# The up-projection with tokens stationary and 512 weight columns moving, block borders crossed one token tile at a time, and the modulation tiles spread anew

## The reference, cut to what matters

```
cond = silu(c)
mod  = (cond @ ada_w[layer] + ada_b[layer]).reshape(B, 9, 1024)
h = modulate(rmsnorm(x, g), sh, sc)
x = x + 0.5 * gate * swiglu(h, w13, w2)     # D_FF = 2816, four times in all
x = x + gate2 * mix                         # layer 0: attention, layer 1: pooling
```

## Time and profile before

| quantity | value |
|---|---|
| span of the profiled execution | 1045.7 us |
| time of that execution | 1047.53 us |
| median of the runs | 1046.29 us |
| PE busy | 955.1 us (91%) |
| DVE busy | 739.9 us (71%) |
| ACT busy | 434.0 us |
| POOL busy | 123.0 us |
| share of PE in the chain that ended last | 82% |
| mean DMA rate | 229 GB/s |

### The profile page before, as it was taken

One profiled execution on the slowest core, in us unless ns is written; L12 is line 12 of the kernel. 1 busy time (PEld: TensorE's weight loads), 2 busy tenths in 40 slices (PEclk: granted clock), 3 DMA queues, 4 the chain that ended last, 5 costly groups with the idle time before them and its releaser, 6 DMA issues.

```text
span 1045.7 us, 15095 instructions
## 1 busy us (share of the span) xinstructions
PE 955.1 (91%) x6240; PEld 866.6 (83%) x6240; DVE 739.9 (71%) x791; ACT 434.0 (42%) x529; POOL 123.0 (12%) x182
## 2 busy tenths in 40 slices
PE   1599999998979597999999989999999879999997
PEld 1499999986857466999999979999998779999996
DVE  4888787857897846887878478878784675454543
ACT  1343434443526544444443344343443445434341
POOL 1111111002451102111110021101110010000000
PEclk9999999998989788999999989999999889999999
DMA  9989888867624106899797567989794225564621
GB/s 339 373 306 327 305 313 291 298 177 234 231 96 153 40 2 228 281 331 345 272 324 261 192 221 258 330 284 333 265 346 158 81 82 198 184 198 165 215 67 61
DMA packets 147140, 239.58 MB, mean 229 GB/s; under 512 B 16128, under 2 KB 108160, under 8 KB 146944
## 3 DMA queue, kind: packets, MB, share of 16 engines
q1 hardware_dynamic: 126480, 166.81, 48.2%
q0 software_dynamic: 19440, 71.31, 17.7%
q10 hardware_dynamic: 1152, 0.49, 0.2%
HBM read 237.54 MB, written 1.05 MB: 228 GB/s over the span
## 4 chain that ended last, share of the span: by engine, by line
PE 82%; DVE 11%; ACT 2%; issue 2%; POOL 1%; DMA 1%; POOLq 0%; ACTq 0%; SPq 0%; DVEq 0%
PE ps L1151 55%; PE ps L1193 7%; PE ps L1194 7%; PE ps L1197 7%; DVE x L814 1%; DVE xn L810 1%; DVE lo L722 1%; PE ps L1213 1%; PE ps L1206 1%; DVE acc L768 1%; DMA x<-in_x 1%; POOL rstd L385 1%; DVE xn L768 1%; PE ps L1443 1%; DVE arena L944 1%
## 5 line engine op out<-in xcount | busy, mean ns | idle before, releaser
L1151 PE MATMUL ps<-hT_hi,hi 128*128 128x256 f32 x1408 | 405.2, 288 | 4.4 <-DVE hT_lo L831 4.4
L1151 PE MATMUL ps<-hT_lo,hi 128*128 128x256 f32 x1408 | 401.8, 285 | 0.0
L1151 PE MATMUL ps<-hT_hi,lo 128*128 128x256 f32 x1408 | 401.6, 285 | 0.0
L722 DVE TENSOR_TENSOR lo<-raw,hi 128x2048 fp32r<-128x2048 f32 (+1 forms) x110 | 244.3, 2221 | 126.1 <-ACT hi L461 125.7
L1151 PEld LDWEIGHTS ps<-hT_hi,hi 128*128 128x128 f32 x1408 | 273.5, 194 | 9.4 <-issue 7.1
L1151 PEld LDWEIGHTS ps<-hT_lo,hi 128*128 128x128 f32 x1408 | 273.6, 194 | 3.5 <-issue 1.2
L461 ACT ACTIVATE hi<-raw 128x2048 fp32r<-128x2048 f32 (+1 forms) x106 | 200.6, 1892 | 181.9 <-PE ps L1151 165.0
L1151 PEld LDWEIGHTS ps<-hT_hi,lo 128*128 128x128 f32 x1408 | 273.3, 194 | 0.0
L1193 PE MATMUL ps<-hi,u_hi 128*128 128x512 f32 x344 | 135.3, 393 | 2.8 <-DVE u_lo L742 2.6
L1194 PE MATMUL ps<-lo,u_hi 128*128 128x512 f32 x344 | 135.2, 393 | 0.0
L368 POOL DMA_DIRECT2D ada<-in_ada_w x132 | 71.6, 543 | 439.7 <-DVE acc L768 160.6
(11 more groups left out here) (138 smaller groups left out, 823.6 us busy)
## 6 DMA issues: line engine op xcount, KB each, us to landing
raw<-in_ff_w SPq DMA_DIRECT2D x264, 512.0 KB, 6.5
ada<-in_ada_w POOLq DMA_DIRECT2D x132, 512.0 KB, 7.1
raw<-in_w_in SPq DMA_DIRECT2D x24, 512.0 KB, 5.0
arena<-in_ada_w SPq DMA_DIRECT2D x4, 1024.0 KB, 18.9
raw<-in_w_out SPq DMA_DIRECT2D x8, 512.0 KB, 4.4
raw<-in_ada_w SPq DMA_DIRECT2D x2, 1024.0 KB, 15.1
arena<-in_b_rpb SPq DMA_DIRECT2D x16, 128.0 KB, 4.7
x<-in_x SPq DMA_DIRECT2D x2, 512.0 KB, 7.5
```

The costliest lines, as they stand in the source:

```text
L722: ins = V.tensor_tensor(lo, src, hi.bitcast(F32), ALU.subtract)
L1151: ins = mm(out, a, b, start=first and m == 0, stop=last and m == len(pairs) - 1, skip_group_check=shared)
```

## The change

The change has six parts.

1. `w13` now holds 128 tokens stationary (`hT`) and moves 512 weight columns, 256 of each half of the SwiGLU (two runs in the piece). A piece takes 24 products of 128 x 512 instead of 48 of 128 x 256. Since the result now has the tokens on the partitions, `u` must be transposed: `u_transpose` adds four 128 x 128 transposes per pair, and the split of `u` reads PSUM.
2. The last pair of a block is done tile by tile: w13 and w2 of tile 0, then its residual and norm while TensorE works on tile 1. The first pair of the next block starts with tile 0, and tile 1's norm transposes stand within it. The mixer's input projection and the output projection are ordered likewise.
3. `lo` is written over `raw`, `hi13` has four slots and the pieces seven (three of them in the arena while it is idle). A slot is reloaded once TensorE has used the piece. `raw2` and `hi2` have four slots.
4. The modulation tiles: block 0 takes 40 in pairs 1 to 9, block 1 takes 40 in pairs 2 to 9 (five a pair), block 2 takes 32, block 3 the last 8. The sums are transposed in two halves in one bank.
5. Of the first 16 tiles TensorE takes four as products with a column of `cond` (`mod_columns`), and VectorE twelve, the last two in halves.
6. The eight GpSimd instructions on the bias are gone; a 128 x 64 window is built at the start, and VectorE applies it with one minimum per token tile (`bias_window`) at steps 10 and 11 of the input projection.

```diff
-                for kk in range(4):
-                    k = 4 * half + kk
-                    hh, hl = hT_hi[:, k, :], hT_lo[:, k, :]
-                    for ab in range(2):
-                        for q in range(2):
-                            ins = three(dst, ((wh, hh), (wh, hl), (wl, hh)), k == 0 and q == 0, k == KT - 1, shared=True)
+                for t in tiles:
+                    tok = slice(t * P, (t + 1) * P)
+                    for kk in range(4):
+                        k = 4 * half + kk
+                        hh, hl = hT_hi[:, k, tok], hT_lo[:, k, tok]
+                        ins = three(ps[:, pair_bank(f, p) + t, :].rearrange("p (m c) -> p m c", m=2),
+                                    ((hh, wh[:, :, kk, :]), (hh, wl[:, :, kk, :]), (hl, wh[:, :, kk, :])),
+                                    k == 0, k == KT - 1)
...
+            def u_transpose(f, p, tiles=range(TT)):
+                for t in tiles:
+                    for q in range(2):
+                        dst = ps[:, z + t, q * P:(q + 1) * P] if last else ps[:, z, q * 256 + t * P:q * 256 + t * P + P]
+                        ins = nc.tensor.transpose(dst, u_buf[:, t, q * P:(q + 1) * P], ident[:, :])
...
+                    w13(f, p, 0)
+                    u_transpose(f, p - 1)
+                    w13(f, p, 1)
+                    w2(Q0 + 2 * p - 2)
+                    w2(Q0 + 2 * p - 1)
...
+                w13(f, LAST, 0, [0])
+                u_transpose(f, LAST - 1)
+                w13(f, LAST, 1, [0])
+                w2(Q0 + NC - 4, tiles=[0], done=None)
+                u_transpose(f, LAST, [0])
+                w2(Q0 + NC - 3, tiles=[0], done=None)
+                w2(Q0 + NC - 2, tiles=[0], done=None)
+                w2(Q0 + NC - 1, tiles=[0], last=True, done=y0_done)
+                w13(f, LAST, 0, [1])
+                w13(f, LAST, 1, [1])
+                    norm_transpose(s_out, 0)
+                w2(Q0 + NC - 4, tiles=[1])
+                u_transpose(f, LAST, [1])
+                w2(Q0 + NC - 3, tiles=[1])
+                w2(Q0 + NC - 2, tiles=[1])
+                w2_last(Q0 + NC - 1)
...
+ADA_COUNT = [{1: 4, 2: 4, 3: 5, 4: 4, 5: 5, 6: 4, 7: 5, 8: 4, 9: 5}, {p: 5 for p in range(2, 10)},
+             {p: 4 for p in range(2, 10)}, {2: 4, 3: 4}]
+PE_TILES = ((5, 7), (3, 5))
...
+            def bias_window(t):
+                b = bias[:, t, :, :, :].rearrange("p h r c -> p (h r) c")
+                V.tensor_tensor(b, b, window[:, :].unsqueeze(1).to_broadcast([P, B_HEADS * ROWS, GRID_W]), ALU.min
+                                ).then_inc(bias_done, 1)
-                    nc.gpsimd.affine_select(out=low, in_=low, compare_op=ALU.is_ge, fill=NEG,
-                    nc.gpsimd.affine_select(out=high, in_=high, compare_op=ALU.is_ge, fill=NEG,
```

More of the change, by code:

```diff
@@ L269, in load_win @@
[L269 to L279, removed]
@@ new lines, in load_piece, with load_until @@
+            def load_piece(n):
+                if BEFORE[n] >= 0:
+                    sp.wait_ge(unit_used, BEFORE[n] + 1)
+                for m, src in enumerate(piece_srcs(n)):
+                    rows, cols = src.shape[1:]
+                    c0 = m * rows * cols
+                    sp.dma_start(unit_src(n)[0][:, c0:c0 + rows * cols].rearrange("p (k c) -> p k c", c=cols), src
+                                 ).then_inc(raw13_in[SLOT[n]], 16)
+            loaded = [4]
+            def load_until(n):
+                while loaded[0] < PIECES and BEFORE[loaded[0]] <= n:
+                    load_piece(loaded[0])
+                    loaded[0] += 1
@@ L286, in load_w2 @@
             def load_w2(f, q):
                 n = NC * f + q
[L288 to L297, removed]
+                if n >= 4:
+                    sp.wait_ge(w2_used, n - 3)
@@ L780, in diag, with mod_out @@
+            def mod_out(g):
+                for half in range(2):
+                    mod_half(g, half, MOD_BANK + half)
             def diag(g, k, scale, dst=diag_buf):
@@ L1128, in _ @@
             split_lo(2 * FFN_PAIR[3] + 1)
+            norm_split(5, 0)
+            residual(5, 1, unit_used, 2 * POOL_PAIR + 2, part=1)
+            norm_scale(5, 1)
+            norm_split(5, 1)
             ffn(3)
-            residual(6, w2_used, 4 * NC, halves=4)
         @block.tensor
@@ L1243, in ffn @@
-                if f < 3:
-                    mod_sum(FFN_MODS[f] + 4, spare_bank(f, PAIRS - 1))
-                w2(Q0 + 20, tiles=[0], done=None)
-                w2(Q0 + 21, tiles=[0], last=True, done=y0_done)
-                w2(Q0 + 20, tiles=[1])
-                w2_last(Q0 + 21)
+                Q0, s_in, s_out = NC * f, SUB_OF_FFN[f], SUB_OF_FFN[f] + 1
+                for t in range(TT):
+                    w13(f, 0, 0, [t])
+                    w13(f, 0, 1, [t], between=(lambda: norm_transpose(s_in, 1)) if f and t == 0 else None)
@@ new lines, in ffn, with pool_average @@
+                w2(Q0 + NC - 2, tiles=[1])
+                w2_last(Q0 + NC - 1)
+            def pool_average(kt, first, last):
+                for j in range(first, last):
+                    t0 = kt * (P - max(WINDOWS) // 2)
+                    c0 = (j % 2) * 256
+                    ins = mm(ps[:, POOL_BANK[j // 2], c0 + t0:c0 + SEQ], xn[:, kt, j * P:(j + 1) * P],
+                             avg[:, j // 2, kt, t0:], start=kt == 0 and j % 2 == 0, stop=kt == 1, skip_group_check=True)
+                    if j % 2 and kt:
+                        ins.then_inc(pool_ps, 1)
@@ L1278, in proj @@
                         t0_done = None
+                    if between is not None and kk == 1:
+                        between()
                 if done:
@@ L1374, in _ @@
             n0 = 2 * WIN_PAIR
+            for t in range(TT):
+                for w in range(2):
+                    proj(n0 + w, lambda t: ps[:, 4 + t, :], tiles=[t], hs=lambda t, k: HLO[1] + 8 * t + k + 1,
+                         start=w == 0, stop=w == 1, done=t == 1, t0_done=seg_ps if (t, w) == (0, 1) else None,
+                         between=(lambda: norm_transpose(1, 1)) if (t, w) == (0, 1) else None)
             for w in range(12):
```

996 lines of the change are left out of this document (585 added, 411 removed).

## The result

| kernel | median of the runs | ratio to before, 95% interval |
|---|---|---|
| before | 1046.7 us (4 runs) | 1 |
| after | 1018.2 us (1016.1 to 1021.4, 4 runs) | 0.9742 (0.9716 to 0.9768) |

The change made the kernel 2.6% faster. My sum had 1010.0 us for the profiled execution; it took 1016.1, with a span of 1014.0. The median lies 9.7 us above my 1008.5. That is inside the whole range (994 to 1027), but at its own forecast's upper edge: 1018.2 stands just outside both 1001 to 1017 and 1000 to 1018. Stretch by stretch, all but one came within 1.6 us of the forecast, and the mixer's early stretch missed it by 9.8. First the busy time by stretch, of the kernel after, with the columns of the earlier trace rows: us, PE, PEld, DVE, ACT, POOL, granted clock, DMA share, GB/s.

What follows compares the result with a forecast made beforehand. TensorE was taken to bound the blocks, with gains also at borders and in the mixer. Terms summed to 37.5 us off the profiled 1047.5, so 1010.0; median forecast 1008.5 us, whole range 994 to 1027.

Steps and rivals of the forecast that it cites:

- 1001 to 1017 and 1000 to 1018: Kernel time in us: the forecast case, given chance 0.60, and the likeliest case's own range.
- the mixer's early stretch: Mixer from the end of its first two pieces to the piece behind the first scores: 54.8 us before, gain 11.5.
- TensorE's pace in the blocks: Blocks' middle pairs: w13 products 0.227 us each, a pair 16.9 us instead of 17.0, gain 2.3 us.
- rival 1: Blocks: w13's two-run operand costs as much as two products, 1035.5 us; chance 0.09 together with slower transposes of u, 1030.5.
- The transposes of `u`: Each pair in the blocks: four transposes of u inside the running stream cost about 0.48 us.
- Rivals 2 and 3: 2: VectorE or modulation-tile ring bounds blocks 0 and 1, 1025, chance 0.10; 3: u's round trip stands bare, 1056, 0.05.
- the borders: Block 0 to mixer, block 1 to 2, mixer to block 1, block 2 to 3: gains of 7.3, 7.7, 3.3, 4.0 us.
- the start: Program start: four tiles leave VectorE, the first weights' DMA and last tiles set the pace; gain 1.3 us.
- TensorE's own work in it is 41.9 ... 43.3: a gain of 11.5: Mixer up to the scores: without GpSimd's slowing VectorE is no later than TensorE; 54.8 us falls to 43.3.
- stays above 50 us: Sign that the prediction is wrong: the mixer's stretch to the scores stays above 50 us.
- The minima: Mixer: VectorE's two minima over 2048 elements replace GpSimd's cuts and cost 1.1 us.

Runs made afterwards that it cites:

- experiment 5: Kernel after, with each of the four transposes of u in a pair done twice: 1035.8 us, ratio 0.9907.
- Experiment 6: Kernel after, with tile 1's w13 again ahead of tile 0's w2 products in a block's last pair: 1040.6 us, ratio 0.9957.
- experiments 9 and 10: Kernel after with early bias loads and block 3's first split later: 1009.3 us; the same without modulation tiles on TensorE: 1012.6 us.
- experiment 3: Kernel after with early bias loads, the eight bias cuts back on GpSimd and VectorE's minima gone: 1020.0 us, ratio 0.9748.
- experiments 1 and 2: Kernel after, 1: bias table's loads issued early, ahead of the mixer's weight pieces, 1012.1 us; 2: those loads left out, 1012.7 us. Both ratio 0.9682.
- experiment 4: Kernel after, with SyncE issuing each pair's two w2 chunks ahead of the w13 pieces: 1059.2 us, ratio 1.0130.

## Why the prediction was right, and where it was not

**Right: TensorE's pace in the blocks.** 24 products of 512 columns take 5.44 to 5.49 us a piece, 0.227 each, with the moving operand in two runs: rival 1 is out. The transposes of `u` cost 0.44 us for four where I had 0.48. That rests on experiment 5, not on the trace alone. The Trainium skill ("TensorE: Matmul & The Clock Gate", Part 4, PE-mode transpose) has about 275 ns for one transpose in another kernel; here, between products, it is 0.11 us, and the measurement decides. Rivals 2 and 3 did not come about: TensorE is busy 141.0 of 141.0 us in block 1. Rival 2 has one trace in block 0: the wait of 2.2 us at 103.08 is for VectorE's part of a modulation sum.

**Right: the borders.** 7.6, 7.9, 3.9 and 3.6 us, against 7.3, 7.7, 3.3 and 4.0. Experiment 6 shows that the cover under tile 1's w13 carries it. Inside the sum two sizes were off and nearly cancelled: the wait before tile 1's transposes is 0.74 us where I had 2, and tile 0's is 0.49; TensorE's own work is 37.0 us of the 38.2 where I had 36.5.

**Right in size, too sure in kind: the start.** It gave 1.2 of 1.3 us. The first weights' transfer stands in the chain up to 29.70, but VectorE's last tiles stand in it behind the first split, so both set the start. The edit's own part I had from the DMA side alone; experiments 9 and 10 show 1.2 us of it at the start.

**Wrong: "TensorE's own work in it is 41.9 ... 43.3: a gain of 11.5".** The step said that without the slowing VectorE would be no later than TensorE, and it left the third partner out, the queue that brings the weights. The stretch took 53.1 us. Part 6 of the change did its work: the slowing costs 9.9 us in the profile, and 7.9 in the medians, where it is put back (experiment 3). The Trainium skill ("SBUF — State Buffer", Who interferes with whom) says that a VectorE instruction with two SBUF inputs contends with a GpSimd instruction that reads SBUF. This agrees with it: the forms slowed in experiment 3 are of that kind.

But SyncE's loads had moved too. Before, the sixteen bias loads were issued ahead of the mixer's last sixteen transfers of `w_in` (from 221.42, 15.44 us of issuing); now two stand behind each piece's load. Their place gives back 6.9 us in the profile and 6 in the medians (experiments 1 and 2). That a slot is now reloaded only once TensorE has used it was not tested by itself. I had counted the DMA's bytes for the blocks only, and never the order in the queue for the mixer, though the diff shows it. My own mark for failure, "stays above 50 us", was met.

With the loads early the stretch is 46.2 us, and 2.9 us of my term stay short: TensorE waits 1.1 for splits and 2.1 for ScalarE's copies, where I had put 1.4 for the copies alone. That makes 1.9 of the 2.9; some of the rest is in pieces after such waits (5.72 us at 292.41). The chain of experiment 1 comes to that stretch's last wait for a split by a modulation tile's transfer (6.76 us at 256.05) and GpSimd's root over 128 x 16 (5.00 us at 270.43, where the same form takes 2.90 at 317.72), so these are what ends last there next. All this is read from the profile, and was not tested by itself.

**Minima and middle pairs.** The minima cost nothing visible where I had 1.1 (experiment 3). The middle pairs gave 3.9 and not 2.3, though block 0's lost 1.1. The wait of 2.2 us at 103.08, with a DMA share of 1.06 from 100 to 105, is more than that loss. What it comes from was not settled: experiment 4 only showed that w2 ahead of w13 is no cure.

**The sum.** 37.5 us forecast; 31.7 measured, made of 9.8 less in the mixer and 4.0 more elsewhere. That the total came out this near is in part luck: the 4.0 us were not foreseen, and without them the median would be about 1022, well outside the forecast's own range.

## What to carry to other kernels

When a change takes one delay off a stretch, write down for all three partners (engine, other engines, DMA queue) what comes next there; count a transfer by how long it holds its queue and how full it makes the engines, not by its bytes. Where a load waits for a buffer, everything behind it in that queue waits as well, so loads whose buffers are free go first. And put small scattered loads where the weights are already ahead.

## What the runs showed of the hardware

- With loads of 128 KB in runs of 256 bytes between the weight pieces, the DMA engines had a busy share of 1.15 at 242 GB/s; without them the same window had 0.65 at 210. The pieces between them landed in 10.2 us (median) instead of 5.1.
- GpSimd's cuts slow VectorE by form (experiment 3): 2.2 to 3.4 times for a product of two operands of 128 x 512, 1.65 times for a split of 128 x 2048, and 5.8 times for an addition of 8 columns (0.98 us where it takes 0.17). It also goes the other way: beside a VectorE minimum of 128 x 2048 that had started first, a GpSimd instruction over 128 x 16 took 2.17 us instead of 0.20.
- TensorE can pay a wait twice: behind 2.59 us of idle a piece took 8.60 us instead of 5.49 (experiment 3), and behind 5.93 us eight transposes took 1.97 instead of 1.09 (experiment 6), both at a granted clock of 0.50.
- A 128 x 128 transpose in the middle of products costs 0.11 us at full clock (experiment 5; granted clock 1.00 in block 1).
